# A two-block transformer kernel: the first head group's inversion inside the preparation, and the adaLN sums closed a pair of tiles later

## The reference, cut to what matters

```python
for l in range(DEPTH):                      # DEPTH = 2
    mod = c_act @ w_ada[l] + b_ada[l]       # adaLN: six vectors of 1024 for layer l
    ...
    o_dn = gated_delta_rule_chunked(dq, dk, dv, g, beta)
    ...
    x = x + gt1 * (merged @ w_o[l])
    ...
    x = x + gt2 * ((jax.nn.silu(up_act) * up_lin) @ w_down[l])

# in gated_delta_rule_chunked, for every head and chunk:
    L = jnp.where(tri_strict, einsum(k_beta, kc) * decay, 0.0)
    A = L + jnp.eye(C)
    sol = triangular_solve(A, rhs, lower=True, unit_diagonal=True)
    qk = einsum(qc, kc) * decay
    def step(S, xs): ...                    # the recurrence over chunks, with S the state
```

## Time and profile before

| what | value |
|---|---|
| median of 3 runs | 2744.89 us (2741.3 to 2747.51) |
| profiled execution, its own time | 2751.09 us |
| its span, first to last instruction | 2749.1 us |
| mean granted clock of TensorE | 0.969 |
| busy: TensorE matmul, weight load | 93%, 75% |
| busy: VectorE, ScalarE, GpSimd | 53%, 39%, 33% |
| one preparation step of the delta rule on TensorE | 5.9 us |

### The profile page before, as it was taken

One profiled execution on the slowest core, in us unless ns is written; L12 is line 12 of the kernel. 1 busy time (PEld: TensorE's weight loads), 2 busy tenths in 40 slices (PEclk: granted clock), 3 DMA queues, 4 the chain that ended last, 5 costly groups with the idle time before them and its releaser, 6 DMA issues. The chain is left out here.

```text
span 2749.1 us, 33369 instructions
## 1 busy us (share of the span) xinstructions
PE 2558.3 (93%) x13185; PEld 2054.3 (75%) x13185; DVE 1451.3 (53%) x2548; ACT 1075.6 (39%) x1872; POOL 915.0 (33%) x400
## 2 busy tenths in 40 slices
PE   5989998999989999989998989999999998999998
PEld 3767767897867888766776767877788886786787
DVE  6299649554645545545994562354444206736323
ACT  3445464245332332133554533543323223336432
POOL 1532232112434444335222221134344443332343
PEclk9999999899999999999999989999999998999999
DMA  7221325643233436532222153322223333831232
GB/s 252 63 71 53 123 69 155 179 138 131 92 112 133 143 102 206 179 116 66 73 76 97 51 119 89 122 89 92 77 93 106 94 98 112 153 115 51 73 122 77
DMA packets 331390, 300.00 MB, mean 109 GB/s; under 512 B 56718, under 2 KB 302820, under 8 KB 330212
## 3 DMA queue, kind: packets, MB, share of 16 engines
q1 hardware_dynamic: 279268, 279.52, 32.6%
q10 hardware_dynamic: 51968, 18.35, 2.6%
HBM read 267.92 MB, written 29.93 MB: 108 GB/s over the span
## 5 line engine op out<-in xcount | busy, mean ns | idle before, releaser
L275 PE MATMUL ps<-hh,split 128*128 128x512 f32 x3808 | 1289.0, 406 | 28.0 <-POOL split L222 17.3
L222 POOL TENSOR_TENSOR split<-ring,split 128x1024 fp32r<-128x1024 f32 (+2 forms) x340 | 808.1, 2378 | 1387.7 <-ACT split L218 1348.0
L275 PEld LDWEIGHTS ps<-hh,split 128*128 128x128 f32 x3808 | 727.3, 191 | 200.2 <-POOL split L222 31.3
L275 PE MATMUL ps<-hl,split 128*128 128x512 f32 x1904 | 752.1, 395 | 0.0
L218 ACT ACTIVATE split<-ring 128x1024 fp32r<-128x1024 f32 (+1 forms) x336 | 341.5, 1018 | 879.7 <-PE ps L275 678.3
L275 PEld LDWEIGHTS ps<-hl,split 128*128 128x128 f32 x1904 | 364.5, 191 | 73.1 <-issue 8.4
L275 PE MATMUL ps<-split 128*128 128x512 f32 x1152 | 283.9, 404 | 8.9 <-DVE split L1136 7.1
L275 PEld LDWEIGHTS ps<-split 128*128 128x128 f32 x1152 | 217.5, 189 | 70.3 <-issue 14.7
L2264 PE MATMUL ps<-split 128*128 128x512 f32 x1056 | 248.2, 397 | 0.0
L2264 PEld LDWEIGHTS ps<-split 128*128 128x128 f32 x1056 | 202.7, 192 | 42.8
L587 POOL TENSOR_TENSOR split<-ring,split 128x1024 fp32r<-128x1024 f32 x32 | 76.1, 2377 | 326.3 <-ACT split L579 326.3
(11 more groups left out here) (426 smaller groups left out, 3235.2 us busy)
## 6 DMA issues: line engine op xcount, KB each, us to landing
ring<-in_w_in_dram SPq DMA_DIRECT2D x60, 1024.0 KB, 5.2
ring<-in_w_up_dram SPq DMA_DIRECT2D x44, 1024.0 KB, 5.1
ring<-in_w_in_dram SPq DMA_DIRECT2D x34, 512.0 KB, 5.1
big<-in_w_ada_dram SPq DMA_DIRECT2D x16, 1024.0 KB, 8.5
ring<-in_w_ada_dram SPq DMA_DIRECT2D x32, 512.0 KB, 3.6
spare<-in_w_ada_dram SPq DMA_DIRECT2D x16, 1024.0 KB, 7.5
ring<-in_w_down_dram SPq DMA_DIRECT2D x16, 896.0 KB, 5.3
ring<-in_w_swa_out_dram SPq DMA_DIRECT2D x8, 1024.0 KB, 5.3
```

The source lines that it names most:

```text
L222: on.tensor_tensor(halves(pt, nk)[1], slot(n, nk)[:, :, e * P:(e + 1) * P], halves(pt, nk)[0], ALU.subtract).then_inc(low_made, 1)
L275: ins = nc.tensor.matmul(ps[bank[gt]][0:m, :], w[:, k, :], r[:, k, :], start=(k == 0 and w is w_high and r is rhs[0]), stop=(k == nk - 1 a ...
```

## The change

Three things are changed together.

1. `invert` is cut into `invert_begin`, `invert_rows` and `invert_end`. Group 0's inversion stands inside the last two preparation steps on VectorE, two rows after each of the four parts of a step. In these two steps each `fill` writes two units for one, and `GAP` goes from 24 to 16. VectorE makes none of the adaLN adds in them; the recurrence gets eight more, and the numbers of loads and closings follow.
2. On ScalarE's queue `send_low(0)` stands ahead of step 4 and `fetch_blocks(0)` inside step 5. `send_blocks(0)` follows `send_low(1)` at once. `fetch_blocks(1)` stands behind `fetch_inverse(0, 0)`, and group 1's `send_blocks` and `fetch_inverse` stand in the second and third level of the first pair.
3. In layer 0's down projection the closings of tiles 4 and 5 stand one pair later, after the third piece of the pair (j = 1, e = 0) and not the fifth, and so do the next ones; the last two stand at the end, ahead of the sums of squares.

```diff
-                    GAP = 24
+                    GAP, EARLY = 16, NP - 2
-                    ADA_P3, ADA_P4 = 32, 32 + 6 * 12
+                    ADA_P3, ADA_P4 = 24, 24 + 6 * 12
+                    def units(p):
+                        return 2 if p >= EARLY else 1
...
-                            fill(1)
+                            fill(units(p))
...
         ScalarE
                         for p in range(NP):
                             g, c = p // TT, p % TT
+                            if p == TT:
+                                send_low(0)
                             act.wait_ge(d_clamp, p + 1)
...
+                            if p == TT + 1:
+                                fetch_blocks(0)
-                            fill(3)
+                            fill(3 * units(p))
...
-                            fill(1)
-                            if p == TT:
-                                send_low(0)
-                            if p == TT + 1:
-                                fetch_blocks(0)
+                            fill(units(p))
                         send_low(1)
-                        fill(KD)
-                        fetch_blocks(1)
                         send_blocks(0)
                         fill(KD)
                         fetch_inverse(0, 0)
-                        send_blocks(1)
-                        fill(GAP - 2 * KD)
-                        fetch_inverse(1, 0)
+                        fetch_blocks(1)
+                        fill(GAP - KD)
...
                                 fill(2)
+                                if q == 0 and lv == 1:
+                                    send_blocks(1)
+                                if q == 0 and lv == 2:
+                                    fetch_inverse(1, 0)
...
         VectorE
+                        def invert_early(p, n):
+                            if p >= EARLY:
+                                j = 8 * (p - EARLY) + 2 * n
+                                if j == 0:
+                                    invert_begin(0)
+                                invert_rows(0, j, j + 2)
+                                if p == NP - 1 and n == 3:
+                                    invert_end(0)
...
-                            fill(1)
-                            more(1)
+                            invert_early(p, 0)
+                            fill(units(p))
+                            more(1 if p < EARLY else 0)
...
-                        invert(0)
                         fill(KD)
-                        invert(1)
+                        invert_begin(1)
+                        invert_rows(1, 0, SUB - 1)
+                        invert_end(1)
                         fill(GAP - KD)
...
                                 fill(1)
-                                more(1)
+                                more(2)
...
         down projection, TensorE
-                                        if l + 1 < DEPTH and j == 2 and e == 0:
-                                            for m in (4 + k, 5 + k):
-                                                close_first(pe, m)
+                                        if l + 1 < DEPTH and k >= 2 and j == 1 and e == 0:
+                                            close_first(pe, 2 + k)
+                                            close_first(pe, 3 + k)
...
+                        if l + 1 < DEPTH:
+                            close_first(pe, 10)
+                            close_first(pe, 11)
                         pe.wait_ge(mix_summed, KD - 2)
```

More of the change, by code:

```diff
@@ L1381, in halves_by @@
                         def halves_by(t):
-                            return min(2 * N_REST, 4 + 2 * t if t < 4 else 10 + 3 * max(0, t - 6))
+                            return min(2 * N_REST, 4 + 2 * t if t < 2 else 8 + 3 * max(0, t - 6))
                         for t in range(NT):
@@ L1737, in open_up_to, with blocks_of, invert_begin, invert_rows @@
                                 open_ += 1
[L1739 to L1742, removed]
+                        def blocks_of(g):
+                            return (b[g].rearrange("p (r c) -> p r c", c=SUB) for b in (sub_a, sub_x, sub_xt, sub_tmp))
+                        def invert_begin(g):
                             dve.wait_ge(l_in, 16 * (g + 1))
                             nc.vector.memset(sub_x[g], 0.0).then_inc(i_step, 1)
-                            dve.wait_ge(i_step, n0 + 1)
+                            dve.wait_ge(i_step, 32 * g + 1)
                             nc.vector.memset(sub_x[g][:, 0:SUB * SUB:SUB + 1], 1.0).then_inc(i_step, 1)
-                            for j in range(SUB - 1):
+                        def invert_rows(g, j0, j1):
+                            a, xx, xt, tmp = blocks_of(g)
+                            for j in range(j0, min(j1, SUB - 1)):
                                 size = [P, SUB - 1 - j, j + 1]
-                                dve.wait_ge(i_step, n0 + 2 * j + 2)
+                                dve.wait_ge(i_step, 32 * g + 2 * j + 2)
                                 nc.vector.tensor_tensor(tmp[:, j + 1:, 0:j + 1],
@@ L1780, in _ @@
                             ins.then_inc(d_low, 1)
-                            fill(1)
-                            more(1)
+                            invert_early(p, 1)
+                            fill(units(p))
+                            more(1 if p < EARLY else 0)
                             dve.wait_ge(d_kq, p + 1)
@@ L1786, in _ @@
                                                            in1=decay(g, c), op0=ALU.mult, op1=ALU.mult).then_inc(d_qk, 1)
-                            fill(1)
-                            more(1)
+                            invert_early(p, 2)
+                            fill(units(p))
+                            more(1 if p < EARLY else 0)
                             dve.wait_ge(d_grow, p + 1)
@@ L1791, in _ @@
                                                            op0=ALU.mult, op1=ALU.mult).then_inc(d_qd, 1)
-                            fill(1)
-                            more(1)
+                            invert_early(p, 3)
+                            fill(units(p))
+                            more(1 if p < EARLY else 0)
                             open_up_to(4 * (p - 1) // KD)
-                        invert(0)
                         fill(KD)
-                        invert(1)
+                        invert_begin(1)
+                        invert_rows(1, 0, SUB - 1)
+                        invert_end(1)
                         fill(GAP - KD)
@@ L1836, in _ @@
                         for c in range(TT):
-                            open_up_to((ADA_P4 + 6 * (c - 1)) // KD if c else (ada_done(3, 2) + 4) // KD)
+                            open_up_to((ADA_P4 + 8 * (c - 1)) // KD if c else (ada_done(3, 2) + 4) // KD)
                             for g in range(2):
```

10 lines of the change are left out of this document (6 added, 4 removed).

## The result

The changed kernel takes 2754.18 us (median of 6 runs, 2749.37 to 2761.71); the kernel before took 2743.59 us beside it (6 runs, 2739.01 to 2747.51). The ratio is 1.0043, with a 95% interval of 1.0031 to 1.0055: the medians stand 10.6 us apart, and the interval of the ratio reaches from 8.5 to 15 us slower (its centre is 11.8, since it isn't the quotient of the two medians). The forecast of 2746.9 is 7.3 us too low; the time lies in the range of 2738 to 2756, near its upper end.

A forecast was written before the change was run, and what follows sets the result against it. TensorE, busy 93% of the span, was taken as the bound, so only its idle and lower-clock time could be won. Terms -2.0 + 4.0 = +2.0 us on the profiled execution gave 2746.9 us on the median; 8-in-10 range 2738 to 2756.

The forecast's parts named there:

- the recounted adds: Eight fewer adaLN adds in the chunks, eight more in the recurrence: costed at nothing; without VectorE's idle cover 4.5 us.
- Part 1: Group 0's inversion moved ahead into the last two chunks, both layers: -2.0 us together, between -6 and +6.
- send to fetch: Pair stage, from sending group 0's inverse to fetching it: 6.2 us in layer 0, 4.5 in layer 1.
- It is not what the stage gets: Pair stage: masks wait behind group 1's inversion, so not 6.7 us but 2.3 (layer 0) and 1.6 (layer 1) are gained.
- the quick rival: Small fetch passes the large one (4.0 us) and the down projection's sums load quickly: 2738 us, chance 0.17.
- one of the prediction's own signs of being wrong: Pair stage: L1508 less than 1 us or more than 5 us earlier against the start of the chunks.
- The term of +1.3 for group 1's fetch: Pair stage: group 1's inverse, fetched in the first pair's third level, makes TensorE wait 1.2 us (layer 1), a few tenths (layer 0).
- Part 2: Down projection between the layers, adaLN closings one pair later: +4.0 us, between -2 and +9.
- The predicted waits: Down projection: TensorE waits 3.4 us at tile 13 and the same at tile 19, released by GpSimd.
- another of the prediction's signs of being wrong: Down projection: the last sum of squares comes earlier than before.
- The rival in which these waits lose the clock: Waits at tiles 13 and 19 exceed 3 us, each followed by a clock drop costing 2.5 to 3: 2754.5, chance 0.27.
- My slow rival: Down projection's new waits each lose the clock, its closings cost +9.5, the moved inversion 0: 2754.5 us, chance 0.27.

The follow-up runs named there:

- e4: Kernel before with only the recounted adaLN adds, loads and closing numbers, inversion and closings unmoved: 2752.75 us, ratio 1.0041 to before.
- e3: Changed kernel with SyncE loading the next projection's first slab ahead of the last four adaLN halves: 2746.03 us, ratio 1.0016 to before.
- e6: e3 with group 1's small fetch issued right behind the sends of group 0's blocks, ahead of the large fetches: 2733.93 us, ratio 0.9972 to before.
- e8: Changed kernel with the slab's load ahead as in e3 and the closings put back: 2741.33 us, ratio 0.9999 to before.
- e1: Kernel before with only the later closings of the adaLN sums: 2746.71 us, ratio 1.0019 to before.
- e2: Changed kernel with the closings put back, leaving the moved inversion and recounted adds and loads: 2752.53 us, ratio 1.0036 to before.
- e5: e1 with the closings one tile earlier, behind the later pair's second tile instead of its third: 2730.75 us, ratio 0.9958 to before.
- e7: Changed kernel with slab's load ahead, small fetch ahead and closings one tile earlier: 2724.77 us, ratio 0.9935 to before.

## Why the prediction was right or wrong

**The step that failed: the recounted adds, costed at nothing.** I argued that a load waits for adds two halves back in both kernels, and that VectorE has time. Both are true, and beside the point. What I left out is the queue of the waiting engine: behind the last gated half, SyncE holds the first slab of the next projection, and behind the high part of that slab ScalarE holds the copy that the recurrence needs. Even the bound I gave (4.5 us if the cover is gone) was the price of the adds, not of a wait passed through two queues. The runs show 10.1 us in the stage (58.0 to 68.1), 10.4 us for the numbers alone (e4), and nothing when only the load's place changes (e3). This term makes the median's loss: without it the forecast's -2.0 + 4.0 stands beside e3's measured +3.6. The measured time lies in the stated range all the same, since the range was made wide for other reasons; that is luck.

**Part 1, the pair stage: the wait that was named came, and the sum was 1.5 to 4 us too good.** The first product came 4.5 us earlier against the start of the chunks (72.1 us behind it for 76.6), where 6.7 were forecast. The mis-sized term is send to fetch: it took 10.1 us in layer 0 and not 6.2, and 7.9 in layer 1 and not 4.5. The send of the transposes landed 9.1 us after its issue, for 5.8 before. It now goes out 2.3 us behind the send of group 1's input, 1 MB on the same queue. In all six kernels with the moved inversion it took 8.9 to 9.2 us in layer 0, in the four others never over 5.8. Group 0's inversion itself was quicker than forecast (it ended at 462.0, not 464.5). "It is not what the stage gets" held: the small fetch, issued at 473.24, 1.1 us behind the first large one, was waited for until 479.21, 7.1 us after that one's issue, where I took 7.3 and the quick rival 4.0.

That is the order in which, by the Trainium skill (page DMA: Bandwidth & Descriptors, section Queues, rings and completion order), the descriptors of one issuing engine's ring are consumed. The traces lean the same way and do not prove it: from its own issue the fetch behind the large ones landed in 5.8 to 6.4 us in four traces (layer 0), group 0's fetch, with nothing large right ahead, in 3.7 to 5.0 in the same four. e6 shows from the other side that the place costs: with the same fetch ahead of the large ones the mask waits of 3.8 and 5.2 us are 0.9 and 1.3.

The first masked product came 0.8 us earlier against the chunks in the two traces, for 2.3 forecast, and layer 1 gained nothing. Less than 1 us was one of the prediction's own signs of being wrong. Over the first eight traces of the table it is 0.1 us earlier in layer 0 and 1.2 later in layer 1. The term of +1.3 for group 1's fetch was too dear: 0.3 us in layer 1 and no wait in layer 0. Over the table, A is 169.4 with the moved inversion against 168.1 as before, D 155.9 against 155.0: a loss of 2.2 us, where I had -2.0. By the medians (e8) it is -0.5, between -3.6 and +3.0. So part 1 without its load wait is worth about nothing, with the sign open. The 168.1 is an average of two kinds of trace, near 166 and near 170; see the last section.

**Part 2: the mechanism right, the size by two errors that cancel.** The forecast was +4.0 (between -2 and +9); e1 measured +4.3 and e3 against e8 +4.1. The predicted waits stand at tiles 13 and 19, though split over two neighbours: 1.20 and 1.87, 0.70 and 2.04 us, in all 5.8 us where 3.4 twice was forecast. VectorE's four half sums took from 1099.04 to 1118.20, 19.2 us for 20.4, and a pair takes 35.5 us (1097.98 to 1133.46) where I had 37.0. So the new stage was forecast too long, by 4.5 us up to the last sum (145.3 for 140.8) and by some 2 for the clock. In these two traces the last sum even came earlier against the stage's start, which was another of the prediction's signs of being wrong. The rival in which these waits lose the clock is refuted: in the traces of after, e1 and e3 the granted clock stays at 1.00 through all of them, as here in a window of the changed kernel over the first two (columns as in the earlier trace rows, the clock is the number ahead of the last two):

```profile
1113.00:1122.00 9.00, 7.01 (x30) 5.12 (x28) 6.11 (x8) 2.80 (x4) 3.72 (x2) 1.00 0.71 247
```

The old stage was too long in my sum as well, by the choice of the trace. The closing waits of 4.9 us with one of 3.38 are not what each execution has. Four traces have the old closings: two show 4.9 us in all, two show 2.1 and 2.4. TensorE's closings in e8, then the last half sum on VectorE in e8 and in e2, each with its wait for the load:

```profile
1100.58 0.95 PE L370 MATMUL ps<-cst,kd 128*128 128x1 f32 x8
1104.92 1.87 PE L370 MATMUL ps<-cst,kd 128*128 128x1 f32 x8 [3.39 <-DVE kd L363]
```

```profile
1099.79 5.07 DVE L363 SCALAR_TENSOR_TENSOR kd<-spare,c_act,kd 128x512 f32<-128x512 f32 x4 [3.20 <-DMA spare<-in_w_ada_dram]
```

```profile
1104.96 3.24 DVE L363 SCALAR_TENSOR_TENSOR kd<-spare,c_act,kd 128x512 f32<-128x512 f32 x4 [2.55 <-DMA spare<-in_w_ada_dram]
```

The same four instructions take 5.07 or 3.24 us, and e2's closing waits 0.60 us. The trace of before had the long case (5.25 us in the earlier trace rows), and its stage C is 3.7 us longer than the average of the four (143.6 for 139.9). Whether a load that lands a little earlier or a GpSimd instruction beside the sums decides between the two was not separated.

The larger part of the spread is the clock. In the trace of before it falls at 1072.6, 1106.7, 1144.2 and 1178.4, each time at a pair of closings, and not only at the one that the prediction names; in the new order it does not fall before the last closings. The whole stage in one window, before and then e4:

```profile
1043.70:1187.30 143.60, 137.26 (x600) 113.02 (x599) 87.54 (x87) 30.18 (x34) 55.58 (x24) 0.94 0.58 196
1052.10:1188.60 136.50, 132.66 (x599) 109.64 (x598) 87.32 (x87) 30.17 (x34) 55.42 (x24) 0.97 0.62 207
```

By mean granted clocks of 0.94, 0.95, 0.96 and 0.97 (before, e8, e2, e4) I estimate 8.6, 7.1, 5.5 and 4.1 us lost to the lower clock. With these and the closing waits of 4.9, 4.9, 2.1 and 2.4 us taken off, the four stages are alike, 130 us, and e5, which has neither, takes 129.4. So part 2 gave up closing waits and slow work, together 6.5 to 13.5 us, for 9.3 us of other waits (5.8, 2.0 and 1.5) and a slow end. The table's C column gives +1.8 us for part 2 and the medians 4.3 and 4.1; the difference is inside their intervals (e1's reaches down to +1.6).

**The sum.** Forecast +2.0; the medians say +10.6: about 10 for the load, some 4 for the closings, and the rest, some -4, is not assigned; 8.5 to 15 is the interval. My slow rival (2754.5) named the right time for a wrong reason: it rested on the clock at tiles 13 and 19.

## What to carry to other kernels

When a change moves the count at which a gate opens, follow the engine that waits at the gate: everything behind the wait in its queue moves too, and then everything behind that on the next engine. Before costing such a step at nothing, look at the idle bracket of the first consumer behind it; "2.64 us, released by this DMA" says that there is no slack. And take a term that rests on one wait of one execution from several traces: here it was 0.6 or 3.4 us from run to run. One tile's difference in where the closings stand (e5 against e1) was worth 12 us in its stage.

## What the runs showed of the hardware

**The lower clock lasts for a varying time after work resumes.** In two traces TensorE comes back from nearly the same idle time before the first product (9.3 us in before, 9.9 in e4). It resumes at 484.17 and 484.88 at 0.50, the 1.2 GHz level. Windows of before, then of e4:

```profile
490.00:492.00 2.00, 2.00 (x11) 1.90 (x9) 0.00 (x0) 0.00 (x0) 0.00 (x0) 0.50 1.11 322
494.00:496.00 2.00, 2.00 (x10) 1.61 (x9) 1.15 (x3) 0.60 (x1) 0.00 (x0) 0.57 0.60 184
```

```profile
490.00:492.00 2.00, 2.00 (x13) 1.72 (x12) 0.69 (x2) 0.00 (x0) 0.00 (x0) 0.76 0.75 226
494.00:496.00 2.00, 2.00 (x17) 1.87 (x16) 0.60 (x2) 0.60 (x1) 0.00 (x0) 1.00 0.63 199
```

e4 is back at 1.00, the 2.4 GHz level, some 6 us after the resumption, before after 11.5. Work at half speed loses half its time, so I estimate that the 5.4 us between them are 2.7 us, most of the 4 us by which A differs in these two. No edit explains it: e1 and e5 have the code of before in this stage, e1 is back after 13.4 us and e5 after 5.9, and their A is 170.5 and 166.1. The Trainium skill (page TensorE: Matmul & The Clock Gate, section What's actually happening) says that the same kernel shows different numbers of slow matmuls at its start from run to run; these rows show the same inside one.

**A second wait and the clock.** In the changed kernel the clock rises while TensorE waits for the mask, and the work behind that wait is slow again; in e6, where the wait is 0.94 us, it rises at about the same time after the first product and stays. Two windows of each, changed kernel first:

```profile
486.00:488.00 2.00, 0.00 (x0) 0.00 (x0) 1.83 (x8) 0.00 (x0) 0.00 (x0) 0.96 0.00 0
490.00:494.00 4.00, 4.00 (x18) 3.60 (x18) 2.60 (x6) 0.60 (x1) 0.00 (x0) 0.50 0.30 86
```

```profile
488.00:490.00 2.00, 1.15 (x10) 1.16 (x11) 1.78 (x6) 0.00 (x0) 0.00 (x0) 1.00 0.00 0
490.00:494.00 4.00, 4.00 (x31) 3.67 (x31) 2.50 (x7) 1.20 (x2) 0.00 (x0) 1.00 0.36 107
```

The same 4 us hold 18 matmul records in the one and 31 in the other. But the short wait does not make the difference by itself. e7 has the same code there and a wait of 0.8 us, which ends at 491.6, and its clock is low behind it:

```profile
492.00:496.00 4.00, 4.00 (x21) 4.00 (x21) 2.52 (x7) 0.00 (x0) 0.00 (x0) 0.50 0.00 0
```

What the ten traces show of layer 0 is this. With one idle stretch, or a short second wait, the clock is back for good 6 us after the first product in three traces (e4, e5, e6) and 11.5 to 13.4 us after it in three (before, e1, e7). In the four with a second wait of 3.6 to 3.8 us (after, e2, e3, e8) it takes some 16 us each time, the wait included. So e6's stage A of 163.5 us holds some of this chance. Its waits in the two pair stages are 8.4 us less than e3's in all (14.4 for 22.8, the waits for the inverse among them); what makes up the rest of the 11.5 us between their medians is not shown.
